# Order of VectorE where the down units of an MLP begin: the last hidden output ahead of one weight low part, four sums of the hidden spread between the first copies out of PSUM

## What is computed

```python
def squared_relu_mlp(u, w1, w2):
    return jnp.square(jax.nn.relu(u @ w1)) @ w2

for layer in range(DEPTH):
    ...
    h = h + mix
    h = h + squared_relu_mlp(rms_norm(h, norm_mlp[layer]), mlp_w1[layer], mlp_w2[layer])
```

## Time and profile before

| what | value |
|---|---|
| median of three runs | 2625.72 us (2622.18 to 2634.36) |
| the profiled execution, its own time | 2626.59 us |
| its span, first to last instruction | 2624.8 us |
| TensorE busy | 2527.2 us (96%) |
| VectorE busy | 1785.7 us (68%) |
| MLP of the first layer, turn from up to down | at about 828 to 876 us of the span |
| MLP of the second layer, the same turn | at about 2291 to 2342 us |

### The profile page before, as it was taken

One profiled execution on the slowest core, in us unless ns is written; L12 is line 12 of the kernel. 1 busy time (PEld: TensorE's weight loads), 2 busy tenths in 40 slices (PEclk: granted clock), 3 DMA queues, 4 the chain that ended last, 5 costly groups with the idle time before them and its releaser, 6 DMA issues. The chain is left out here.

```text
span 2624.8 us, 37850 instructions
## 1 busy us (share of the span) xinstructions
PE 2527.2 (96%) x14000; PEld 2049.3 (78%) x14000; DVE 1785.7 (68%) x2826; ACT 1124.4 (43%) x2184; POOL 1174.9 (45%) x889
## 2 busy tenths in 40 slices
PE   8999889999999999999988999999999999999999
PEld 5777667888887878887876688888788888777887
DVE  6554755477678999853059567666546767899993
ACT  4626544253334434323135566666524333433431
POOL 5362666234445444442236444444633444444441
PEclk8999999999999999999987899999999999999999
DMA  4010003224343544230342423222132334354531
GB/s 168 33 49 33 1 1 117 93 81 161 140 169 134 188 170 146 83 127 32 102 118 65 129 59 100 54 54 54 56 125 79 146 135 170 109 209 149 175 125 65
DMA packets 90973, 275.76 MB, mean 105 GB/s; under 512 B 9879, under 2 KB 38935, under 8 KB 76135
## 3 DMA queue, kind: packets, MB, share of 16 engines
q1 hardware_dynamic: 87240, 255.18, 28.4%
q10 hardware_dynamic: 3552, 18.18, 1.8%
HBM read 197.50 MB, written 73.86 MB: 103 GB/s over the span
## 5 line engine op out<-in xcount | busy, mean ns | idle before, releaser
L1582 PE MATMUL ps<-U_hi,RH 128*128 128x512 f32 x912 | 356.7, 391 | 12.5 <-DVE H L905 4.8
L1586 PE MATMUL ps<-U_lo,RH 128*128 128x512 f32 x912 | 355.7, 390 | 0.0
L1587 PE MATMUL ps<-U_hi,RL 128*128 128x512 f32 x912 | 355.6, 390 | 0.0
L1040 POOL TENSOR_TENSOR RL<-RAW,RH 128x512 fp32r<-128x512 f32 x112 | 156.2, 1395 | 395.2 <-ACT RH L744 395.2
L744 ACT ACTIVATE RH<-RAW 128x512 fp32r<-128x512 f32 x280 | 175.5, 628 | 292.8 <-PE ps L1587 285.4
L1533 POOL TENSOR_SCALAR PX<-PX,rinv,GATE 128x640 f32<-128x640 f32 (+7 forms) x256 | 197.8, 783 | 209.0 <-DVE rinv L3303 209.0
L1582 PE MATMUL ps<-U_hi,W_hi 128*128 128x512 f32 (+2 forms) x656 | 261.9, 399 | 13.3 <-DVE U_lo L2805 10.7
L1582 PE MATMUL ps<-SH,RH 128*128 128x512 f32 x656 | 256.8, 392 | 8.2 <-DVE H L905 4.1
L1586 PE MATMUL ps<-U_lo,W_hi 128*128 128x512 f32 (+2 forms) x656 | 258.2, 394 | 0.0
L1587 PE MATMUL ps<-U_hi,W_lo 128*128 128x512 f32 (+2 forms) x656 | 258.1, 393 | 0.0
L1586 PE MATMUL ps<-SL,RH 128*128 128x512 f32 x656 | 255.9, 390 | 0.0
(11 more groups left out here) (390 smaller groups left out, 6005.9 us busy)
## 6 DMA issues: line engine op xcount, KB each, us to landing
W_raw<-in_pieces SPq DMA_DIRECT2D x30, 1024.0 KB, 5.1
RAW<-in_pieces SPq DMA_DIRECT2D x28, 1024.0 KB, 4.9
RAW<-in_pieces SPq DMA_DIRECT2D x56, 512.0 KB, 7.7
hid_d<-HOA SPq DMA_DIRECT2D x24, 1024.0 KB, 3.9
hid_d<-HOB SPq DMA_DIRECT2D x24, 768.0 KB, 5.4
RHA<-hid_d SPq DMA_DIRECT2D x12, 1024.0 KB, 5.1
RHB<-hid_d SPq DMA_DIRECT2D x12, 768.0 KB, 6.6
U_rawh<-hid_d SPq DMA_DIRECT2D x12, 768.0 KB, 4.8
```

The source lines that it names most:

```text
L1040: G_.tensor_tensor(ring(RL[i], n), quarter(n, (B22, B11)[i - 5]), ring(RH[i], n).bitcast(F32), ALU.subtract).then_inc(u_lop.sem, 1)
L1582: m = mm(o, a_hi, b_hi, start=first, stop=False, skip_group_check=again)
L1586: mm(o, a_hi, b_lo, start=False, stop=False, skip_group_check=again)
L1587: return mm(o, a_lo, b_hi, start=False, stop=last, skip_group_check=again)
```

## The change

Only the order of VectorE's list in `mlp_dve` is altered, once in each layer, with `hidden_sums` taken apart into `hidden_sum(u, k)`, k = 0 to 3. No instruction is added or taken away, and none changes its shape. The lists of the other engines are the same.

```diff
-            def hidden_sums(u):
+            def hidden_sum(u, k):
...
             hidden_out(N_UP - 1, 1)
-            unit_low(N_UP, 3)
             sub_low(1, 0)
             hidden_out(N_UP - 1, 2)
-            for i in range(1, 4):
-                sub_low(1, i)
+            sub_low(1, 1)
+            unit_low(N_UP, 3)
+            sub_low(1, 2)
+            sub_low(1, 3)
             unit_low(N_UP, 4)
             dve.wait_ge(*q_lo.at(sub_no(L, 1, 3)))
             collect(0, 0)
-            hidden_sums(N_UP - 1)
+            hidden_sum(N_UP - 1, 0)
+            hidden_sum(N_UP - 1, 1)
             dve.wait_ge(q_lop, 3 * (L + 1))
             for d in range(N_DOWN):
                 for i in range(7):
...
                     if d or i:
                         collect(d, i)
+                    if d == 0 and i in (1, 2):
+                        hidden_sum(N_UP - 1, i + 1)
                     if 1 <= i <= 5 and d + 1 < N_DOWN:
                         unit_low(N_UP + d + 1, i - 1)
```

More of the change, by code:

```diff
@@ L867, in hidden_out, with hidden_sums @@
                 V_.scalar_tensor_tensor(o, o, 0.0, o, ALU.max, ALU.mult).then_inc(f_hid.sem, 1)
-            def hidden_sums(u):
+            def hidden_sum(u, k):
                 gu = N_UP * L + u
                 t = HO[u % 2]
[L873 to L880, removed]
+                if k == 0:
+                    dve.wait_ge(*sq21.at(gu + 1))
+                    dve.wait_ge(*f_hid.at(10 * gu + 6))
+                    V_.tensor_tensor(t[1], H21[:], t[6], ALU.add).then_inc(f_hid.sem, 1)
+                elif k == 1:
+                    V_.tensor_tensor(t[4], t[0], H21[:], ALU.subtract).then_inc(f_hid.sem, 1)
+                elif k == 2:
+                    dve.wait_ge(*f_hid.at(10 * gu + 7))
+                    V_.tensor_tensor(t[2], t[1], t[0], ALU.subtract).then_inc(f_hid.sem, 1)
+                else:
+                    dve.wait_ge(*f_hid.at(10 * gu + 9))
+                    V_.tensor_tensor(t[5], t[3], t[2], ALU.subtract).then_inc(f_hid.sem, 1)
+            def hidden_sums(u):
+                for k in range(4):
+                    hidden_sum(u, k)
             def sub_low(q, i):
```

## The result

| | before | after |
|---|---|---|
| median of eight runs | 2633.07 us (2622.18 to 2636.96) | 2643.05 us (2634.14 to 2646.65) |
| ratio after / before | | 1.0041, 95% interval 1.0022 to 1.0060 |
| span of the profiled execution | 2624.8 us | 2643.2 us |

The change makes the kernel slower by 0.41%, some 10 us (5.8 to 15.8 by the interval). The forecast was slower by 8.3 us, at 2634, with a range from 2626 to 2640. The direction and about the size of the difference were right; the time itself lies 3 us above the range, since the kernel before, run eight times, is at 2633 and not at 2626.

What follows compares the result with a forecast made beforehand. TensorE, busy 96% of the span, was taken as the bound; the later reload adds 4.4 + 1.1 us and the lower clock 2.8, in all 8.3, giving 2634.9, about 2634 on the median, range 2626 to 2640.

Steps and rivals of the forecast that it cites:

- The base: Whole kernel: profiled 2626.59 us plus 8.3 gives 2634.9; the median of three runs is 0.9 below, so about 2634.
- The race of two chains: Up-to-down turn: copies' chain shortened, store-and-reload chain lengthened; reload 17.9 us after the fourth sum, TensorE stalls some 6 us.
- Part 1: Last output ahead of `unit_low(14, 3)`: down unit 0 starts at 2296.0, not 2297.65; 0.4 us gained at product 2.
- the first stalls: TensorE in down unit 0: 0.8 us idle ahead of it, about 1.3 at product 2 and about 1.3 at product 4.
- The term of the first layer: Product 2 of down unit 1, first layer: starts at 865.9, 4.4 us later than 861.50, before the clock's cost.
- The term of the second layer: Product 2 of down unit 1, second layer: 1.8 us later, less 0.7 won back by unit 2, 1.1 us.
- The clock as a loss only: TensorE's lower clock after the 6 us stall: 1.4 us lost per layer (bounds 0 and 1.8), 2.8 in all.
- The rule of the Trainium skill: Fourth sum to reload: about 2.0 us fixed and 436 GB/s give 15.2 us; the prediction kept the rows' 17.9.

Runs made afterwards that it cites:

- two edits on the queue: Kernel after, with H's reload issued ahead of `load_sub(3)` and HOA stored behind the third sum: ratio 0.9996, turns 282.43 and 282.23 us.
- part 2: Kernel after with the last output put back behind `unit_low(N_UP, 3)`, sums still spread: ratio 1.0059, turns 291.19 and 290.12 us.
- part 1: Kernel before with only the last output moved ahead of `unit_low(N_UP, 3)`, four sums together: ratio 1.0011, turns 285.14 and 284.43 us.

## Why the prediction was wrong in its range

Two terms failed, and the mechanism did not. The base of the sum was 7 us too low, which alone took the time out of the range, and the price of the second layer's turn was too small.

**The race of two chains: right.** Forecast: fourth sum at 19.3 us, the reload 17.9 behind it, product 2 of down unit 1 at 38.0 (865.9 - 827.89). Measured: 19.33, 17.8, 37.99, and nearly the same in the second layer. The stall was forecast at 6 us and was 5.8.

**Part 1 and the first stalls: right.** The stalls of 0.8, 1.3 and 1.3 us came at 0.62, 1.13 and 1.22. Nothing of that gain reached the end. One row was misread without harm: around the operation that reads PSUM the prediction has "two weight low parts" of 1.75 us, but the earlier trace rows show one of them and a `sub_low`, both ahead of it.

**The term of the first layer: right.** 4.4 us and 1.4 for the clock, 5.8 in all, against 5.87. The clock cost an estimated 1.5 there: six rows of 0.63 us start 0.43 us apart and not 0.23, and the rows just ahead of and behind them are longer too.

**The term of the second layer: too small.** "1.8 - 0.7 = 1.1 us", with 1.4 for the clock, makes 2.5. Against the trace that I read it was 3.42, since the low clock cost more there than 1.4: ten rows of 0.63 us, from 38.5 to 42.4 us of the turn, against six in the first layer, by the same working an estimated 2.4 us. But against what the kernel before does in the other traces it is 289.72 - 283.0 = 6.7. I took one execution's turn of 286.30 for the kernel's, though its first layer, with the same instructions, took 282.98 right beside it. That the four sums met GpSimd in one layer and not in the other was in the rows, and I used it, but did not ask which of the two was the rule.

**The clock as a loss only: incomplete.** I wrote that the low stretch in the turn of before "lay before the reload and cost nothing at the end". That was said of the stretch behind the 3.25 us stall. Behind the 2.3 us stall a low stretch does more than that: it delays GpSimd and lets VectorE through, and the seven turns that had it came out 3.3 us shorter than the one that had not.

**The base: this took the time out of the range.** The step is "the median of the three runs is 0.9 below it, so about 2634". It took 2625.7 for the kernel before, and eight runs gave 2633.07. The three runs shown spread over 12 us. The larger sets of the kernel before, taken beside the experiments, have their medians at 2629.93, 2629.60 and 2627.78. With 2633.07 as the base the forecast would have been 2641.4, 1.7 us from the result. The difference itself, 9.98 us of medians, stands against 8.3 forecast; typical turns alone (5.9 + 6.7) make 12.6, inside the interval of 5.8 to 15.8. That the sum came out at 8.3, so near the measured difference, is in part luck: it stands on the one turn of 286.30. And the profiled execution of 2626.59 us looked like a fair base because its two oddities nearly cancelled, 4.3 us short ahead of the first turn and 3.3 long in the second; the two other traces of before, with neither, took 2627.46 and 2627.72. The range should have held the spread of the base beside the costs of the change.

**The rule of the Trainium skill** (DMA: Bandwidth & Descriptors, Anatomy of one DMA) would have had the reload at an estimated 15.2 us behind the sum. That fit is for one transfer on another queue, and here the reload waits for a store to land first. The traces of the change show 17.8, so the rows were the better guide. By 15.2 the time would have been at the edge between faster and slower.

## What to carry to other kernels

When operations are moved to feed the busiest engine sooner, look at what else waits for them. Here the last of four moved sums released a store, and behind it, in one full queue, a reload with VectorE's whole list behind it; the change took 0.45 us (first layer) and 2.4 us (second layer, first trace) out of one chain, at product 4, and put up to 5 into the other. When two chains race, look which one ends last before reordering the other. Here two edits on the queue brought the landing 6.0 us sooner and took the loss away, but neither they nor the new order made the kernel measurably faster than before, where in the usual turn VectorE does not wait for the reload at all. And before one trace is taken as the base of a small difference, compare the places that repeat within it: two layers with the same instructions and 3.3 us between them say how much of the difference is luck.

## What the runs showed of the hardware that I had not expected

- A stretch of this kernel was shorter where TensorE's clock had fallen. With the clock down behind a stall of 2.3 us a turn of before took 282.9 to 283.1 us, seven times; with the clock up 286.30, once. No run sets the clock at will, so the cause rests on the rows. They lead over GpSimd, which starts its sums 1.5 us later; VectorE's operations with two operands in SBUF take 0.67 us beside a quiet GpSimd and 1.66 to 1.78 beside a busy one.
- Stalls of 2.28 to 2.33 us at the same place were followed by the lower level in seven turns of eight with the order of before, and in part 2 in one turn of two; the stalls of 2.48 us of part 1 in one turn of two.
- The loss behind the 5.8 us stall was not the same in the two layers of one execution: six matmuls of 0.63 us in the one and ten in the other.
